# Product-key experts: a tile of 128 tokens by gathered rows, 384 tokens dense

## The reference

```python
q = (t @ wq).reshape(ntok, PEER_HEADS, 2, PEER_DH)
sc = jnp.einsum('thpd,hpkd->thpk', q, subkeys)
s1, i1 = lax.top_k(sc[:, :, 0], PEER_TOPK)
s2, i2 = lax.top_k(sc[:, :, 1], PEER_TOPK)
best, pos = lax.top_k(cand, PEER_TOPK)           # cand: all sums s1 + s2
idx = e1 * PEER_NKEYS + e2
gate = jax.nn.softmax(best, axis=-1)
# for each token: its 8 x 16 = 128 experts
act = jax.nn.gelu(jnp.einsum('phkd,pd->phk', u_tab[ib], tb)) * gb
out = jnp.einsum('phk,phkd->pd', act, v_tab[ib])
```

## Time and profile before

| | |
|---|---|
| median of 3 runs | 3645.8 us (3645.3 to 3651.99) |
| the profiled execution | 3639.07 us, its span 3637.2 |
| TensorE busy | 3538.1 us, 97% |
| VectorE busy | 2284.6 us, 63% |
| ScalarE busy | 1472.4 us, 40% |
| GpSimd busy | 884.6 us, 24% |

### The profile page before, as it was taken

One profiled execution on the slowest core, in us unless ns is written; L12 is line 12 of the kernel. 1 busy time (PEld: TensorE's weight loads), 2 busy tenths in 40 slices (PEclk: granted clock), 3 DMA queues, 4 the chain that ended last, 5 costly groups with the idle time before them and its releaser, 6 DMA issues.

```text
span 3637.2 us, 56094 instructions
## 1 busy us (share of the span) xinstructions
PE 3538.1 (97%) x22572; PEld 3247.0 (89%) x22572; DVE 2284.6 (63%) x3965; ACT 1472.4 (40%) x2191; POOL 884.6 (24%) x795
## 2 busy tenths in 40 slices
PE   8999999999899999999998999999999999999998
PEld 8988999999797678788677877899999999999998
DVE  7445465554844545555687444479988885777775
ACT  7254453222625435222466444243333433333333
POOL 4010022111401012211213201035646662111110
PEclk9999999999999999999999999999999999999999
DMA  4212232222221123222222122348869999999894
GB/s 155 70 42 65 76 116 93 93 92 94 70 65 54 63 82 133 95 97 93 75 81 70 60 93 81 95 140 272 281 214 258 298 289 338 314 310 313 307 312 139
DMA packets 293617, 544.70 MB, mean 150 GB/s; under 512 B 138288, under 2 KB 187568, under 8 KB 292976
## 3 DMA queue, kind: packets, MB, share of 16 engines
q1 hardware_dynamic: 185248, 394.34, 32.6%
q0 software_dynamic: 27648, 100.68, 8.4%
q10 hardware_dynamic: 80464, 46.10, 4.3%
HBM read 483.67 MB, written 56.62 MB: 149 GB/s over the span
## 4 chain that ended last, share of the span: by engine, by line
PE 86%; DVE 8%; ACT 3%; issue 1%; POOL 1%; DMA 0%; ACTq 0%; DVEq 0%; POOLq 0%
PE PSM L317 19%; PE PSM L318 18%; PE PSM L319 18%; PE PSM L211 5%; PE PSM L3160 5%; PE PSM L3162 5%; PE PSM L3161 5%; PE PSM L3136 3%; DVE PARTS L284 2%; ACT PARTS L275 1%; PE PSM L1061 1%; DVE MH L1741 1%; PE PSM L825 1%; PE PSM L1097 1%; DVE QK L1375 1%
## 5 line engine op out<-in xcount | busy, mean ns | idle before, releaser
L284 DVE TENSOR_TENSOR PARTS<-RAW,PARTS 128x1024 fp32r<-128x1024 f32 (+1 forms) x612 | 743.8, 1220 | 476.4 <-ACT PARTS L275 476.2
L275 ACT ACTIVATE PARTS<-RAW 128x1024 fp32r<-128x1024 f32 x612 | 645.4, 1057 | 932.1 <-PE PSM L319 488.6
L317 PE MATMUL PSM<-UX,PARTS 128*128 128x264 f32 (+3 forms) x2912 | 987.1, 339 | 27.4 <-DVE UX L2297 4.9
L318 PE MATMUL PSM<-UX,PARTS 128*128 128x264 f32 (+3 forms) x2912 | 970.2, 333 | 0.0
L319 PE MATMUL PSM<-UX,PARTS 128*128 128x264 f32 (+3 forms) x2912 | 969.5, 333 | 0.0
L317 PEld LDWEIGHTS PSM<-UX,PARTS 128*128 128x128 f32 x2912 | 548.8, 188 | 78.4 <-issue 9.2
L318 PEld LDWEIGHTS PSM<-UX,PARTS 128*128 128x128 f32 x2912 | 549.0, 189 | 29.9 <-issue 1.7
L319 PEld LDWEIGHTS PSM<-UX,PARTS 128*128 128x128 f32 x2912 | 547.9, 188 | 29.7
L3160 PE MATMUL PSM<-AC,PARTS 128*128 128x416 f32 x1024 | 358.3, 350 | 2.3 <-DVE AC L3457 2.3
L3162 PE MATMUL PSM<-AC,PARTS 128*128 128x416 f32 x1024 | 357.6, 349 | 0.0
L3161 PE MATMUL PSM<-AC,PARTS 128*128 128x416 f32 x1024 | 357.5, 349 | 0.0
(11 more groups left out here) (516 smaller groups left out, 5815.9 us busy)
## 6 DMA issues: line engine op xcount, KB each, us to landing
RAW<-w_ff_dram SPq DMA_DIRECT2D x128, 512.0 KB, 3.2
RAW<-peer_u_dram SPq DMA_DIRECT2D x128, 512.0 KB, 4.8
RAW<-peer_v_dram SPq DMA_DIRECT2D x128, 512.0 KB, 5.1
RAW<-w_in_dram SPq DMA_DIRECT2D x116, 512.0 KB, 3.2
acts_dram<-MQ ACTq DMA_DIRECT2D x128, 208.0 KB, 4.2
MQ<-acts_dram SPq DMA_DIRECT2D x128, 208.0 KB, 3.8
MQ<-gates_dram SPq DMA_DIRECT2D x128, 208.0 KB, 4.7
RAW<-w_mix_o_dram SPq DMA_DIRECT2D x32, 512.0 KB, 3.3
```

Source lines behind the costliest of these rows:

```text
L275: e.activation(p[:, 0:1024], self.raw.of(i), ACT.Copy).then_inc(S.sem, S.tick("w", i))
L284: e.tensor_tensor(p[:, 1024:1024 + n], r[:, 0:n], p[:, 0:n].bitcast(F), SUB).then_inc(V.sem, V.tick("w", i))
L317: e.matmul(dst, wh[k], xh_[k][:, lo:hi], start=(k == 0), stop=False, skip_group_check=True)
L318: e.matmul(dst, wh[k], xl_[k][:, lo:hi], start=False, stop=False, skip_group_check=True)
```

## The change

All in the expert layer:

- Tokens 384 to 511 (all of token tile 3) are gathered, 128 gathers of u and of v with one token per partition; 384 tokens are dense. The copies across partitions go. The choice is spread over tiles 1 to 72 instead of 1 to 68; the gate stage is tiles 74 to 121, with six fills.
- Dots 0 to 29 keep five buffers, dots 30 to 107 have three (tiles 80 to 126), and the last 20 dots run in the down stage, before the sums, all with seven buffers in the space of the inputs (`late`). Between tiles 6 and 122 of the down stage stand these 20 dots and 128 sums.
- Fills 4 and 5 stay in `Gb`; fills 0 to 3 are stored in pieces of 2 KB and loaded for four tiles at once. `gated` has two instructions, 128 columns from `Gb` and 256 from the loaded ones.
- GpSimd subtracts half of each tile for u tiles 5 to 73 and for v tiles 4 to 127.
- In the gate stage VectorE makes A and B of the first half, ScalarE makes A of the second as relu(1 - |e1 - iota|), and GpSimd makes B of the second, now times the gate.

```diff
-        Gd = nc.dram_tensor("gates_dram", (128, 128, 416), F, kind="Internal").ap()
-        Ad = nc.dram_tensor("acts_dram", (128, 128, 416), F, kind="Internal").ap()
+        Gd = nc.dram_tensor("gates_dram", (4, 128, 128, 64), F, kind="Internal").ap()
+        Ad = nc.dram_tensor("acts_dram", (128, 128, 384), F, kind="Internal").ap()
...
-                self.pooled = {first["pu"] + i for i in range(5, 68)}
+                self.pooled = {first["pu"] + i for i in range(5, 74)} | {first["pd"] + i for i in range(4, 128)}
...
-        TD, FEW, HALVES = 416, 96, 64
+        TD, FEW, LATE = 384, 128, 20
...
-        gv_ = [qb(oGb + 1024 * i, 1024) for i in range(8)]
+        gv_ = [UF[:, 1024 * i:1024 * i + 1024] for i in range(7)]
...
+        kept = MQ[:, oGb:oGb + 16384].rearrange("p (h n t) -> p n h t", h=2, n=128)
...
-        ORDER = [3, 0, 1, 2]
-        HERE = 46
-        FILLS = [(3, 384, 4)] + [(g // 2, 64 * g, 8) for g in range(6)]
-        FILL_AT = [70] + [74 + 8 * g for g in range(6)]
+        ORDER, END = [3, 0, 1, 2], [15, 34, 53, 72]
+        HERE, THERE = 30, FEW - LATE
+        FILLS = [(g // 2, 64 * g, 8) for g in range(6)]
+        FILL_AT = [74 + 8 * g for g in range(6)]
...
-            return 21 + 45 * s_ // (HERE - 1) if s_ < HERE else 77 + 49 * (s_ - HERE) // (FEW - 1 - HERE)
+            return 21 + 50 * s_ // (HERE - 1) if s_ < HERE else 80 + 46 * (s_ - HERE) // (THERE - 1 - HERE)
...
+        def late_by(r):
+            return 6 + 116 * r // (FEW + LATE - 1)
...
         def gates_out(f, c):
-            lo, m = FILLS[f][1], 8 * FILLS[f][2]
-            return (Gd[8 * c:8 * c + 8, :, lo:lo + m].rearrange("n p t -> p n t"), Gb[half_of(f)][:, 8 * c:8 * c + 8, 0:m])
+            return Gd[f, :, 8 * c:8 * c + 8, :], Gb[half_of(f)][:, 8 * c:8 * c + 8, :]
...
                 e.wait_ge(V.sem, V.at("w", iD + i))
+                if iD + i in W.pooled:
+                    e.wait_ge(G.sem, G.at("w", iD + i))
...
+            def one_hots(n, t8):
+                i4 = four_at(n, t8) + 1
...
+                for i in range(4):
+                    e.activation(a[:, 128 * i:128 * i + 128], iota, ACT.Abs, bias=E1[:, t0 + i:t0 + i + 1],
+                                 scale=-1.0).then_inc(S.sem, S.tick("off", i4))
+                e.wait_ge(S.sem, S.at("off", i4))
+                e.activation(a, a, ACT.Relu, bias=con["ones"][:, 0:1], scale=-1.0).then_inc(S.sem, S.tick("onA", i4))
...
             def gated(i):
-                e.wait_ge(ga_in[i % 4], 32 * (i // 4 + 1))
-                x = gact[i % 4][:, 0:TD]
-                e.tensor_tensor(x, x, ggate[i % 4][:, 0:TD], MUL).then_inc(V.sem, V.tick("gated", i))
+                e.wait_ge(ga_in[i % 4], 16 * (i // 4 + 1))
+                x, y = (gact[i % 4][:, 256 * h:256 * h + 256 - 128 * h].rearrange("p (f t) -> p f t", t=64) for h in range(2))
...
+                e.tensor_tensor(y, y, kept[:, i], MUL).then_inc(V.sem, V.tick())
+                e.wait_ge(gg_in[i // 4 % 2], 16 * (i // 8 + 1))
+                e.tensor_tensor(x, x, gate4[i // 4 % 2][:, i % 4], MUL).then_inc(V.sem, V.tick("gated", i))
...
                 for i in range(4):
-                    e.tensor_scalar(o[:, 128 * i:128 * i + 128], iota, E2[:, t0 + i:t0 + i + 1], None,
-                                    ALU.is_equal).then_inc(G.sem, G.tick("onB", i4))
+                    e.tensor_scalar(o[:, 128 * i:128 * i + 128], iota, E2[:, t0 + i:t0 + i + 1], Gt[:, t0 + i:t0 + i + 1],
+                                    ALU.is_equal, MUL).then_inc(G.sem, G.tick("onB", i4))
...
+            for i in range(NB):
+                if iD + i + 2 in W.pooled:
+                    W.pool(e, iD + i + 2)
+                for r in late_gathers_at(i):
...
+                    if r >= LATE + 7:
+                        e.wait_ge(V.sem, V.at("sum", r - LATE - 7))
+                    elif r >= 7:
+                        e.wait_ge(V.sem, V.at("dot", THERE + r - 7))
```

202 lines of the change are left out of this document (95 added, 107 removed).

## The result

| | median us | lowest to highest | runs |
|---|---|---|---|
| before | 3648.98 | 3642.2 to 3651.99 | 11 |
| changed | 3667.62 | 3655.63 to 3677.51 | 11 |

The ratio is 1.0055, with a 95% interval of 1.0045 to 1.0066. The changed kernel is slower by 0.55%, where 2.1% less was forecast. The profiled run of the changed kernel took 3672.2 us with a span of 3670.4.

What follows compares the result with a forecast made beforehand. TensorE was taken as the bound, by its matmuls' number and spacing. From 3639.1 us, saving 93 gave 3546; adding 5, 3, 9 and 1.5 gave 3564.5, and 6.7 for the median gave 3571 us, range 3552 to 3606.

Steps and rivals of the forecast that it cites:

- The pitch: Dense matmuls of 384 instead of 416 columns: starts 0.173 us apart instead of 0.1864, -83 us.
- the blocks: Gate stage: 48 blocks of 16 gate matmul records instead of 52, each 1.78 us of TensorE, -7 us.
- the seam: Between up and down stage: shorter wait before the first down matmul and no slow clock behind it, -3 us.
- +9 forecast: Gate stage: 6.13 us a tile taken, the middle of 5.93 to 6.4, over 46 tiles.
- The one-hot on GpSimd also gets a second operation ... I take 0.: Gate stage: multiplying by the gate in GpSimd's one-hot costs 0, within bounds of 0 to 0.6 us.
- Rival 4: Gate stage: the second operation on GpSimd repeats the pass, 2.4 us more a tile, +110 us, 3681 us; chance 0.03.
- About 5.95 against 5.93.: Gate stage: GpSimd's one-hots and gathers take about 5.95 us a tile against TensorE's 5.93.
- rival 2: Gate stage set by the three-buffer loop: 6.27 us a tile or more, +16 to +22 and more; chance 0.14.
- +8 forecast: Down stage: +5 us for VectorE held up by GpSimd's half subtraction and +3 us for late loads.
- rival 1: Down stage set by VectorE and GpSimd, or by transfers: 4.33 to 4.46 us a tile, +21 to +36; chance 0.22.
- 0.98 in place of the 0.54 that it saves: Down stage: GpSimd's half subtraction costs VectorE 0.98 us, against 0.54 saved, whenever VectorE has work queued.
- The +3 us for late loads: Down stage: 367 GB/s wanted, so some loads come late, +3 us; at 342 GB/s it would be +36 us.

Runs made afterwards that it cites:

- the fastest kernel: Changed kernel with 49 instead of 20 row products put off to the down stage and GpSimd only gathering (no one-hots, no down-stage halves): 3553.05 us, ratio 0.9735.
- the order turned: Kernel where GpSimd only gathers and 20 row products are put off, with VectorE's gate-stage one-hots made ahead of its row products: 3555.70 us.

## Why the prediction was wrong

**Right: what TensorE saves.** The pitch, the blocks and the seam came out nearly as worked: 0.1736 us, -18.6 us over tiles 8 to 68 (60 x 0.325 = 19.5 were due), 5.99 us for a gate tile of TensorE's own where 5.93 was worked out, 4.16 for a down tile, 3 us at the seam. The sum without any adder was 3546 + 6.7 = 3553 us, and the kernel in which no other engine is late took 3553.05. That they meet within 0.1 us is luck. The spans of the profiled runs of the two kernels, 3637.2 and 3552.6, lie 84.6 us apart where 93 were due; tiles 0 to 8, which took 6 us each before, gave 0.8 us instead of 8 x 0.325 = 2.6, and the gate tiles 0.05 us each less than worked out. The other way, the end from down tile 122 on gave 5.2 us in the changed kernel, of which its tiles account for 2; what is made there besides was put at nought. Five runs of the fastest kernel spread over 8 us.

**Wrong: the gate stage, +9 forecast and 46 x (7.59 - 5.93) = +76 measured.** Two steps failed, the first with 46 x 0.81 = 37 of the 67 us missed and the second with 46 x (6.78 - 6.13) = 30.
- *"The one-hot on GpSimd also gets a second operation ... I take 0."* It costs 0.19 us at least and 0.37 us on average, 1.5 us of GpSimd's time a tile where it has room, and its removal gave back 0.81 us of the tile. The reason I gave, that 128 columns cost nearly what the fixed part costs, came from VectorE's and GpSimd's two-input instructions and not from a row of this form. By "GPSIMD Engine Reference", section 3.1, of the Trainium skill one and two operations per element cost the same on this engine. For this instruction the runs show 0.591 against 0.782 us for the shortest of each. All are of 128 columns, so it stays open whether the 0.19 us are per element, which is what the page speaks of, or per instruction. Rival 4 had the mechanism, with a full repeat of 0.6 us and a chance of 0.03; its test (over 0.8 us undisturbed) was set too high, since it takes less than that to fill a queue with no room.
- *"About 5.95 against 5.93."* The sum put GpSimd within 0.02 us of TensorE's tile and priced the crossing at the middle of a small range. Measured are 4.91 us of one-hots where "some 3.7" stood, and 2.77 of gathers with their gaps where 2.25 stood. The mean of 0.82 us in the earlier trace rows was already 0.22 above the undisturbed time, which was VectorE in its way. I raised it only to 0.92 for the longer dots, though 1.70 row products a tile instead of one met more of the one-hots: 1.01 us on average with one operation and 1.23 with two.

The three buffers, rival 2, were there too, at 0.19 to 0.25 us a tile (6.24 against 6.05 with the order turned and 5.99 with 49 put off), but as the lesser part.

**Wrong: the down stage, +8 forecast and 116 x (4.503 - 4.15) = +41 measured.** The place and the mechanism were those of the text and of rival 1, VectorE blocked by GpSimd's half. The size of one step was off. *"0.98 in place of the 0.54 that it saves"* came from a half that nothing preceded, with an upper bound of 1.14. Over all halves of the changed kernel it is 1.38 on average, 1.54 where the half runs right behind a gather and did not wait. With VectorE's 3.19, which the run without halves bears out (324.2 / 360 x 4.16 = 3.75, less 0.54 = 3.21), that makes 4.57 against the 4.503 measured. The row had been read rightly for its own place. What I missed is that the change puts a gather right ahead of nearly every half (58 of 61), which its order of instructions on GpSimd shows plainly. The run without gathers puts 31 of the 33 us missed down to this. The bound of 1.14 was then no bound. "SBUF — State Buffer", section "SBUF: two separate sides", of the Trainium skill says that the pair of ports is held for the whole instruction and the loser fully blocks. The halves without gathers nearly agree (1.08 us lost for a run of 1.29), and the page was nearer than the value I took: by it the time would have been some 16 us above the one I took, of the 33 that the stage missed by.

**Not there.** The +3 us for late loads: the fastest kernel moved 397 GB/s at a share of 1.03 with TensorE full. The +1.5 us before the gates was about right (TensorE was busy for 227.6 of 230 us).

**The chances.** Each adder was priced as if the others were at their middle, and the range ended where two rivals held at once. The slower side got 0.03, although the text had three engines within 5% of each other in the down stage and two in the gate stage. The two stages missed by 67 and 33 us, together 100, and the whole by 97. The granted clock was 0.94 in the gate stage instead of 1.00; TensorE is not on the chain there, so this is not what the tile took.
